# A ring of weight chunks in on-chip memory, laid out in the order 1, 2, 3, 0

## The chip, the cores and the metric

One core of a Trainium2 chip runs the kernel. The metric is the device time of one execution, in microseconds (us). TensorE is the matmul engine (PE in the profile, PEld its weight loads), VectorE is DVE, ScalarE is ACT, GpSimd is POOL, SyncE is SP.

## What is computed

A decoder block on 512 tokens (16 meta tokens go ahead, 528 in all) with model width 2048, all float32:

```
hn   = rms_norm(h)                       # 528 x 2048
proj = hn @ w_in                         # q k v z, b and a logits, p, gate_a gate_b
q, k, v = silu(conv(q, k, v)); gated delta rule over 8 heads -> o;  y_a = (norm(o) * silu(z)) @ w_proj_a
y_b  = (causal pools of p, mixed by pool_w, scaled) @ w_proj_b
h   += (sigmoid(gate_a) * y_a + sigmoid(gate_b) * y_b) @ w_out
h   += (silu(rms_norm(h) @ w_gate) * (rms_norm(h) @ w_up)) @ w_down
out  = rms_norm(h) of the 512 real tokens
```

## The kernel before

Each large product is made of three matmuls, since a float32 operand is split into two parts, a high one rounded to the fp32r type and a low one that holds the rest: high x high, high x low, low x high. The weights are the stationary operand of the projections; the tokens stream past them.

The token tiles are hn_hi and hn_lo, each [128, 16, 528] (16 tiles kt of 128 model channels, 528 tokens, lines 206 and 207). They lie behind each other from hn_at; one tile is 528 x 4 = 2112 bytes in each partition.

The projection weights come in chunks of 1024 floats a partition: 4 kt tiles x 256 output columns. A chunk passes through three places with four slots each (SLOTS = 4, the slot is the chunk's number modulo 4): SyncE loads it to w_raw (line 520), ScalarE copies it rounded to w_hi (line 935), VectorE subtracts w_hi from w_raw and writes w_lo (line 1378), TensorE reads w_hi and w_lo. When it is done with a chunk (the semaphore chunk_used) the slot is free. Chunk c of a unit of 256 output columns holds the tiles kt = c, c + 4, c + 8, c + 12. It gives 24 groups of work: 2 halves m of 128 output columns, 4 tiles, 3 products.

What TensorE does, in order, with the ring:

- the first unit of stage a (first_unit, line 2105), all chunks first with tokens 0 to 255 (256 columns), then, behind ab_products (line 2170, the same pairs of token parts with a stationary tile of 32 columns, ab_hl, which steps by 128 bytes from one kt to the next, from a multiple of 256 on), all chunks with tokens 256 to 527 (272 columns)
- stage a: 11 more units (q, k, v), chunk_products at line 2128; each weight tile meets the 256 and then the 272 columns (hn_halves)
- the gates: 16 units, real tokens only, 512 columns that begin 16 floats into a token tile (hn_real); pieces of eight such matmuls alternate with the small matmuls of the delta rule
- stage p: 4 units, 256 and 272 columns again
- stage z: 4 units, 512 columns
- the merge: 8 units of 4 chunks, 512 columns of o and zb. Its chunks are written to other tiles over the same memory, w_hi_m and w_lo_m (lines 1097, 1138, 1660, 1794). The tiles of o and zb begin at multiples of 256 bytes.

Later stages use the same memory for other tiles: out (its weights stream, line 2432 to 2434), the FFN (lines 2457 to 2459, 44 units of 7 products of 24 matmuls; weights hi_a, hi_b, hi_c and their low parts stand, the sums s_hi and s_lo with 256 columns stream, from s_at = hn_at + 64) and down. The weights of the FFN's third product, hi_2 and lo_2, begin at ext_at + 8192 from the fifth unit on and 64 bytes behind it in the first four (`two_at`, line 331). The asserts at lines 191, 209 and 219 say that whi_at, wlo_at, hn_at and ext_at are equal modulo 256 (BEAT).

The positions in the ring are set by the function ring. Before, slot i of w_hi begins at whi_at + 64 + 4160 i, slot i of w_hi_m at whi_at + 4096 i, and the same for w_lo.

Of the kernel before, what the change touches and what calls it, by code (L numbers as in the profile page):

```python
# [10 lines left out]
F32R = mybir.dt.float32r  # L11
# [3 lines left out]
P = 128  # L15
# [22 lines left out]
SLOTS = 4  # L38
CHUNK = 1024
# [101 lines left out]
def hybrid_block(nc, x, meta_tokens, norm_mix_w, w_in, conv_w, a_log, dt_bias, o_norm_w, w_proj_a, pool_w,  # L141
                 pool_scale, w_proj_b, w_out, norm_ffn_w, w_ffn_gate, w_ffn_up, w_ffn_down, norm_final_w, out):
    ctx = ExitStack()
    with ctx:
# [12 lines left out]
        top = [(nc.sbuf_base + 63) // 64 * 64]  # L157

        def place(name, shape, dtype=F32, at=None):
            size = int(np.prod(shape[1:])) * 4  # L160
            offset = top[0] if at is None else at
            if at is None:
                top[0] += (size + 63) // 64 * 64
            return nc.alloc_sbuf_tensor_at(name, shape, dtype, offset=offset)
# [2 lines left out]
        raw = [place(f"w_raw{i}", [P, CHUNK]) for i in range(SLOTS)]  # L167


        def ring(name, step, first):  # L170
            return [place(f"{name}{i}", [P, CHUNK], F32R, at=top[0] + first + (4 * CHUNK + step) * i) for i in range(SLOTS)]

        LINE = 64
        whi_at = top[0]
        whi, whi_m = ring("w_hi", LINE, LINE), ring("w_hi_m", 0, 0)
        top[0] += SLOTS * (4 * CHUNK + LINE)
        wlo_at = top[0]
        wlo, wlo_m = ring("w_lo", LINE, LINE), ring("w_lo_m", 0, 0)
        top[0] += SLOTS * (4 * CHUNK + LINE)

        minus_half = place("minus_half", [P, 16])
# [2335 lines left out]
```

## Time and profile before

| | us |
|---|---|
| median of 3 runs (2654.24 to 2655.65) | 2654.39 |
| the profiled execution | 2655.96 |
| its span | 2654.2 |
| TensorE busy | 2604.5 |
| VectorE busy | 1816.0 |
| ScalarE busy | 999.0 |
| GpSimd busy | 318.9 |

The span runs from the first to the last instruction. Matmuls overlap: one is on record for longer than the distance to the next (0.28 us of 256 columns, of which the next begins after 0.11 to 0.12), so the distance between starts is what counts. In the timeline, equal neighbours are merged: x2 is one of 256 and one of 272 columns.

### The profile page before, as it was taken

What the parts mean: (1) busy time and instruction counts of PE and PEld (TensorE: products, weight loads), DVE (VectorE), ACT (ScalarE), POOL (GpSimd) and SP (SyncE); (2) the same over time, 40 slices, a digit from 0 to 9 for tenths busy, and PEclk for the clock granted to TensorE, in tenths of its full rate; (3) what the DMA queues carried; (4) which work ended last, traced back from release to release, by engine and by line L of the source; (5) the groups of instructions that cost most, each with busy time, mean ns of one, the idle gap of its engine ahead of it and who ended that gap; (6) DMA issues with size and microseconds to landing.
All of it is one profiled execution on the core that took longest, in us unless ns stands there. A gap on an engine that the chain in (4) does not pass through costs nothing.

```text
span 2654.2 us, 43654 instructions
## 1 busy us (share of the span) xinstructions
PE 2604.5 (98%) x17278; PEld 2369.4 (89%) x17278; DVE 1816.0 (68%) x1714; ACT 999.0 (38%) x1016; POOL 318.9 (12%) x326
## 2 busy tenths in 40 slices
PE   7999999999999999999989999999999999999998
PEld 6999988888889977888879999999999998888886
DVE  5444555554543234558888888888888888888898
ACT  4443322222222232223454444444444444333334
POOL 6000034444431500100000000000000000000000
PEclk8999999999999999999999999999999999999999
DMA  4333333333333434689333444544454449866562
GB/s 145 98 87 95 84 87 88 91 83 91 88 90 92 110 87 165 231 282 324 127 138 124 161 155 148 173 153 156 147 179 150 154 150 344 279 198 218 161 203 102
DMA packets 346856, 400.84 MB, mean 151 GB/s; under 512 B 11626, under 2 KB 300563, under 8 KB 345619
## 3 DMA queue, kind: packets, MB, share of 16 engines
q1 hardware_dynamic: 287122, 335.39, 40.4%
q10 hardware_dynamic: 59664, 64.51, 7.1%
q8 instruction: 46, 0.75, 0.1%
q14 instruction: 24, 0.19, 0.0%
HBM read 328.02 MB, written 71.84 MB: 151 GB/s over the span
## 4 chain that ended last, share of the span: by engine, by line
PE 92%; DVE 3%; issue 1%; ACT 1%; DMA 1%; POOL 1%; SPq 0%; DVEq 0%; ACTq 0%; POOLq 0%
PE psum L2128 34%; PE psum L2457 10%; PE psum L2459 10%; PE psum L2458 10%; PE psum L2432 7%; PE psum L2433 6%; PE psum L2434 6%; PE psum L2286 2%; PE psum L2105 1%; PE psum L2297 1%; DMA w_raw<-in_w_proj_a 1%; PE psum L2372 1%; PE psum L2267 0%; DMA dn_raw<-in_w_ffn_down 0%; POOL hn_lo L766 0%
## 5 line engine op out<-in xcount | busy, mean ns | idle before, releaser
L2128 PE MATMUL psum<-hn_hi,w_hi 128*128 128x256 f32 (+1 forms) x1600 | 451.2, 331 | 0.0
L2128 PE MATMUL psum<-hn_lo,w_hi 128*128 128x256 f32 (+1 forms) x1600 | 450.0, 330 | 0.0
L2128 PE MATMUL psum<-hn_hi,w_lo 128*128 128x256 f32 (+1 forms) x1600 | 449.3, 330 | 0.0
L1378 DVE TENSOR_TENSOR w_lo<-w_raw,w_hi 128x1024 fp32r<-128x1024 f32 x144 | 190.1, 1321 | 260.7 <-ACT w_hi L935 259.7
L935 ACT ACTIVATE w_hi<-w_raw 128x1024 fp32r<-128x1024 f32 x144 | 152.2, 1058 | 415.8 <-PE psum L2128 387.6
L2128 PEld LDWEIGHTS psum<-hn_hi,w_hi 128*128 128x128 f32 x1600 | 271.0, 188 | 22.8 <-issue 0.2
L2128 PEld LDWEIGHTS psum<-hn_lo,w_hi 128*128 128x128 f32 x1600 | 270.8, 188 | 22.9 <-issue 0.7
L2128 PEld LDWEIGHTS psum<-hn_hi,w_lo 128*128 128x128 f32 x1600 | 270.5, 188 | 22.7
L2432 PE MATMUL psum<-dn_hi,act_hl 128*128 128x512 f32 x616 | 240.9, 391 | 2.0 <-DVE dn_lo L1712 2.0
L2434 PE MATMUL psum<-dn_hi,act_hl 128*128 128x512 f32 x616 | 240.3, 390 | 0.0
L2433 PE MATMUL psum<-dn_lo,act_hl 128*128 128x512 f32 x616 | 240.2, 390 | 0.0
L2457 PE MATMUL psum<-s_hi,hi_a 128*128 128x256 f32 x704 | 194.6, 276 | 1.0 <-DVE s_lo L1883 1.0
L2458 PE MATMUL psum<-s_lo,hi_a 128*128 128x256 f32 x704 | 194.4, 276 | 0.0
L2459 PE MATMUL psum<-s_hi,lo_a 128*128 128x256 f32 x704 | 194.4, 276 | 0.0
L2459 PE MATMUL psum<-s_hi,lo_b 128*128 128x256 f32 x704 | 194.4, 276 | 0.0
L2458 PE MATMUL psum<-s_lo,hi_c 128*128 128x256 f32 x704 | 194.4, 276 | 0.0
L2459 PE MATMUL psum<-s_hi,lo_c 128*128 128x256 f32 x704 | 194.4, 276 | 0.0
L2458 PE MATMUL psum<-s_lo,hi_b 128*128 128x256 f32 x704 | 194.4, 276 | 0.0
L2457 PE MATMUL psum<-s_hi,hi_c 128*128 128x256 f32 x704 | 194.4, 276 | 0.0
L2457 PE MATMUL psum<-s_hi,hi_b 128*128 128x256 f32 x704 | 194.4, 276 | 0.0
L920 POOL TENSOR_TENSOR rms<-rms_a,minus_half 128x1 f32<-128x1 f32 x4 | 2.6, 658 | 1281.9 <-DVE rms_a L2025 1281.9
L1185 ACT ACTIVATE hi<-t 128x1024 fp32r<-128x1024 f32 x44 | 46.8, 1064 | 267.9 <-DVE t L1829 267.9
(359 smaller groups left out, 6236.0 us busy)
## 6 DMA issues: line engine op xcount, KB each, us to landing
w_raw<-in_w_in SPq DMA_DIRECT2D x144, 512.0 KB, 3.9
ffn_raw<-in_w_ffn_gate SPq DMA_DIRECT2D x44, 1024.0 KB, 6.4
ffn_raw<-in_w_ffn_up SPq DMA_DIRECT2D x44, 1024.0 KB, 6.9
dn_raw<-in_w_ffn_down SPq DMA_DIRECT2D x32, 1024.0 KB, 8.3
act_hl<-act_dram SPq DMA_DIRECT2D x56, 512.0 KB, 9.1
act_dram<-comb_hi ACTq DMA_DIRECT2D x22, 896.0 KB, 4.2
act_dram<-comb_lo ACTq DMA_DIRECT2D x22, 896.0 KB, 6.2
out_raw<-in_w_out SPq DMA_DIRECT2D x16, 1024.0 KB, 10.9
```

The source lines that it names most:

```text
L935: act.activation(whi[s][:], raw[s][:], ACT.Copy).then_inc(S["hi_ready"], 1)
L1185: act.activation(two(hi_2s, n)[:], two(t2s, n)[:], ACT.Copy).then_inc(S["hi_ready"], 1)
L1378: dve.tensor_tensor(wlo[s][:], raw[s][:], whi[s][:].bitcast(F32), ALU.subtract).then_inc(S["lo_ready"], 1)
L2105: ins = pe.matmul(outs(m)[i], lhs, mv, start=kt == 0 and j == 0, stop=kt == KT - 1 and j == 2)
L2128: ins = pe.matmul(o, lhs, r, start=kt == 0 and i == 0, stop=kt == 4 * n_chunks - 1 and i == 2)
L2286: ins = pe.matmul(bank(1)[:, i, :], x[:, i, :], B[11][:, i, :], start=True, stop=True)
L2432: pe.matmul(out, a_hi, w_hi, start=start and i == 0, stop=False, skip_group_check=True)
L2433: pe.matmul(out, a_hi, w_lo, start=False, stop=False, skip_group_check=True)
L2434: ins = pe.matmul(out, a_lo, w_hi, start=False, skip_group_check=True, stop=i == k - 1 and (what in ("b21", "b22", "t4") or at_end and wha ...
L2457: pe.matmul(out, w_hi[:, k0 + k, :], s_hi[c][:, k, :], start=start and k == 0, stop=False, skip_group_check=True)
L2458: pe.matmul(out, w_hi[:, k0 + k, :], s_lo[c][:, k, :], start=False, stop=False, skip_group_check=True)
L2459: ins = pe.matmul(out, w_lo[:, k0 + k, :], s_hi[c][:, k, :], start=False, stop=stop and k == HEADS - 1, skip_group_check=True)
```

## The change

The function ring takes a list of four places instead of a step and a first offset. Modulo 256, the slots 0, 1, 2, 3 of w_hi and w_lo begin at 64, 128, 192, 0 before and at 192, 0, 64, 128 after. In memory the order of the slots is 1, 2, 3, 0 after. The tiles of the merge take the same order, at multiples of 256 bytes. No instruction is added, taken away or moved.

```diff
-        def ring(name, step, first):
-            return [place(f"{name}{i}", [P, CHUNK], F32R, at=top[0] + first + (4 * CHUNK + step) * i) for i in range(SLOTS)]
+        def ring(name, places):
+            return [place(f"{name}{i}", [P, CHUNK], F32R, at=top[0] + at) for i, at in enumerate(places)]
 
         LINE = 64
+        BEHIND = [(4 * CHUNK + LINE) * ((i + SLOTS - 1) % SLOTS) for i in range(SLOTS)]
+        EVEN = [3 * (4 * CHUNK) + 4 * LINE, 0, 4 * CHUNK, 2 * (4 * CHUNK)]
         whi_at = top[0]
-        whi, whi_m = ring("w_hi", LINE, LINE), ring("w_hi_m", 0, 0)
+        whi, whi_m = ring("w_hi", BEHIND), ring("w_hi_m", EVEN)
         top[0] += SLOTS * (4 * CHUNK + LINE)
         wlo_at = top[0]
-        wlo, wlo_m = ring("w_lo", LINE, LINE), ring("w_lo_m", 0, 0)
+        wlo, wlo_m = ring("w_lo", BEHIND), ring("w_lo_m", EVEN)
         top[0] += SLOTS * (4 * CHUNK + LINE)
```

## Rows read from the trace of the kernel before

**Rows 1.** The page: span, busy time of PE, granted clock in 40 slices.
```profile
span 2654.2 us, 43654 instructions
...
PE 2604.5 (98%) x17278; PEld 2369.4 (89%) x17278; DVE 1816.0 (68%) x1714; ACT 999.0 (38%) x1016; POOL 318.9 (12%) x326
...
PEclk8999999999999999999999999999999999999999
```

**Rows 2.** PE's waits from 68 to 1018 us (in total, times, longest).
```profile
PE psum L2286 <- DVE gdn L1582: 1.7, 1, 1.7
```

**Rows 3.** SP's longest wait; DVE's split (busy, mean ns, idle before it).
```profile
SPq L520 <- DVE w_lo L1378: 859.6, 142, 19.1
...
L1378 DVE TENSOR_TENSOR w_lo<-w_raw,w_hi 128x1024 fp32r<-128x1024 f32 x144 | 190.1, 1321 | 260.7 <-ACT w_hi L935 259.7
```

**Rows 4.** Groups of PE instructions by form; one of three products each.
```profile
L2128 PE MATMUL psum<-hn_hi,w_hi 128*128 128x512 f32 x640 | 256.8, 401 | 0.0
...
L2128 PE MATMUL psum<-hn_hi,w_hi 128*128 128x272 f32 x480 | 138.2, 288 | 0.0
...
L2128 PE MATMUL psum<-hn_hi,w_hi 128*128 128x256 f32 x480 | 134.1, 279 | 0.0
```

**Rows 5.** The chain that ended last: start us, us, what and how many.
```profile
47.49 7.70 PE psum L2170 x64
55.19 11.87 PE psum L2105 x96
...
68.27 215.55 PE psum L2128 x1792
```

**Rows 6.** The weight loads of L2128, one of three products.
```profile
L2128 PEld LDWEIGHTS psum<-hn_hi,w_hi 128*128 128x128 f32 x1600 | 271.0, 188 | 22.8 <-issue 0.2
```

**Rows 7.** Timeline of PE in the FFN's fourth unit: start us, length us.
```profile
1441.86 0.28 PE L2457 MATMUL psum<-s_hi,hi 128*128 128x256 f32 x1
...
1444.74 0.28 PE L2457 MATMUL psum<-s_hi,hi_b 128*128 128x256 f32 x1
...
1447.46 0.28 PE L2457 MATMUL psum<-s_hi,hi_b 128*128 128x256 f32 x1
```

**Rows 8.** The same in the fifth unit.
```profile
1461.06 0.28 PE L2457 MATMUL psum<-s_hi,hi 128*128 128x256 f32 x1
...
1463.78 0.28 PE L2457 MATMUL psum<-s_hi,hi_b 128*128 128x256 f32 x1
```

**Rows 9.** Timeline of PE in the first unit, last chunk, 256 columns.
```profile
45.17 0.28 PE L2105 MATMUL psum<-hn_hi,w_lo 128*128 128x256 f32 x1
...
47.21 0.28 PE L2105 MATMUL psum<-hn_hi,w_lo 128*128 128x256 f32 x1
```

**Rows 10.** L2128 alone in stage p: stretch, its length, PE busy (count).
```profile
823.70:916.10 92.40, 92.37 (x768) 1.00 0.40 108
```

**Rows 11.** Timeline of PE, ab_products, first matmul of kt = 4 to 8.
```profile
49.24 0.41 PE L2170 MATMUL psum<-hn_hi,ab_hl 128*32 128x256 f32 x2
...
49.73 0.40 PE L2170 MATMUL psum<-hn_hi,ab_hl 128*32 128x256 f32 x2
...
50.20 0.40 PE L2170 MATMUL psum<-hn_hi,ab_hl 128*32 128x256 f32 x2
...
50.69 0.40 PE L2170 MATMUL psum<-hn_hi,ab_hl 128*32 128x256 f32 x2
...
51.17 0.40 PE L2170 MATMUL psum<-hn_hi,ab_hl 128*32 128x256 f32 x2
```

**Rows 12.** Timeline of PE in stage z, before and behind a chunk's boundary.
```profile
918.18 0.39 PE L2128 MATMUL psum<-hn_hi,w_hi 128*128 128x512 f32 x1
...
921.58 0.39 PE L2128 MATMUL psum<-hn_hi,w_hi 128*128 128x512 f32 x1
...
924.34 0.39 PE L2128 MATMUL psum<-hn_hi,w_hi 128*128 128x512 f32 x1
```

## The prediction

> **What bounds the kernel now.** I read the page first, then TensorE's waits, then the spacing of matmuls inside single stages. The page has TensorE at 98% of the span, and the granted clock at its upper level (2.4 GHz) in all but the first slice [rows 1]. Between 68 and 1018 us, where every matmul that the change touches lies except the first unit, TensorE waits once, 1.7 us, for something the change doesn't touch [rows 2]. The engines that fill the ring have room: SyncE waited 860 us in all for w_lo before its loads, VectorE stood idle 260 us before its split [rows 3]. So the number to read is the spacing of consecutive matmuls. A saved or lost nanosecond there goes straight into the time, and nothing else on the path moves.
>
> Three forms of L2128 read the ring through whi and wlo: 640 x 3 matmuls of 512 columns (gates and z), and 480 x 3 each of 272 and of 256 columns, always in pairs (a and p) [rows 4]. With the first unit (L2105, 96 of 256 and 96 of 272 columns) that is 1920 wide ones, 1440 pairs and 192 single ones.
>
> I call **position** the start of a weight chunk minus the start of the token columns that stream during its use, modulo 256 bytes. A token tile has 528 floats, 2112 bytes, so tile kt begins 64 kt past hn_at. Chunk c holds tiles c, c+4, c+8, c+12, which all begin at 64 c. Columns and k blocks inside a chunk step by 512 and 1024 bytes and change nothing. Before, chunk c begins at 64 (c+1): position +64 for a, p and the first unit, and 0 for gates and z, whose columns begin 16 floats later. After, chunk c begins at 64 (c+3), that is 64 (c-1): position -64 for a and p, and 128 for gates and z. The merge tiles begin at multiples of 4096, or at 12544 = 49 x 256, so they stay at position 0. Each matmul has a weight load beside it [rows 6]; only this relation can change its speed, since shapes, counts, order, waits and DMAs are the same.
>
> **What the trace says about positions, at 256 columns.** The FFN shows the clean contrast. In the fourth unit the product of hi_2 uses tiles that begin 64 bytes past a multiple of 256, like the sums s: position 0. Its 24 matmuls take 1444.74 - 1441.86 = 2.88 us, 120.0 ns each; the 24 of hi_b behind them, at -64, take 2.72 us, 113.3 ns [rows 7]. One unit on, the same product reads tiles that begin at a multiple of 256, position -64, and takes 1463.78 - 1461.06 = 2.72 us, 113.3 ns [rows 8]. So position 0 costs 6.7 ns a matmul of 256 columns. Position +64 is in the first unit: 18 steps from 45.17 to 47.21, 113.3 ns [rows 9]. Hence -64 and +64 are equally good at 256 columns, and 0 is bad. Of 128 no row of full width tells.
>
> The Trainium skill (TensorE: Matmul & The Clock Gate, section Part 2: What happens when you issue a matmul) speaks against any effect: TensorE has two independent SBUF read ports, so loading the next tile's weights takes no read bandwidth from the running matmul. By that rule each term below is 0 and the time stays. Rows 7 and 8 disagree with its letter, 120.0 against 113.3 ns for the same line; for the terms below it happens to give the same sum.
>
> **Part 1, a and p: +64 to -64.** Stage a takes 215.55 us for 1792 matmuls, 240.6 ns a pair [rows 5]; stage p has 92.37 us for 384 pairs, 240.5 ns [rows 10]. At the FFN's rate (113.3 / 256 = 0.4427 ns a column) a pair of 528 columns would take 233.8 ns. So 6.8 ns a pair are over, 9.8 us in all, and the first unit's 272-column part (11.87 us / 96 = 123.6 ns [rows 5] against 120.4) has 0.3 us more. Does position hold them? The row nearest to this is ab_products, L2170: the same 256 + 272 pairs on the same tokens, with a load of 32 columns only and a position that walks through 0, 64, 128 and 192 with kt. It takes 7.70 us / 32 = 240.6 ns a pair [rows 5], as much as stage a to a tenth of a nanosecond, and its groups of two pairs take 0.49, 0.47, 0.49 and 0.48 us [rows 11]. With a quarter of the load and every position the excess is the same; it looks like a matter of alternating 256 and 272 columns. Value taken: 0. Bounds: -10.1 us (all of the excess goes), and above nothing: the group at 192 (that is -64) took 10 ns more than the one at 64, 5 ns a pair, 7.2 us for 1440 pairs. The reading is rounded to 10 ns, so it is a bound, not a value.
>
> **Part 2, gates and z: 0 to 128.** At position 0 a matmul of 512 columns, locked in, takes (921.58 - 918.18) / 15 = 226.7 ns [rows 12], exactly twice 113.3. So it shows none of the 6.7 ns that 256 columns pay at the same position. The simplest reading: a conflict delays the weight load, which fills the whole matmul at 256 columns and has half of it to spare at 512. Then 128, whether good or bad for the load, is hidden as well. Value taken: 0. Behind a chunk's boundary the spacing wobbles: (924.34 - 921.58) / 12 = 230.0 ns [rows 12], some 40 ns a chunk. Were that gone in all 80 chunks, -3.2 us. Upper bound: the 6.7 ns of rows 7 on each of 1920, +12.9 us. It isn't hidden by anything if the stream itself is what is delayed, since TensorE is the bound there.
>
> **Part 3, the rest: 0.** Scalar and vector splits write the same 1024 columns to other addresses and have room [rows 3]. The merge tiles only swap places. Loads go to raw, which doesn't move.
>
> **Sum.** The profiled execution took 2655.96 us, span 2654.2 and 1.8 around it, 1.6 above the median of 2654.39. 0 + 0 + 0 leaves 2655.96 for it and 2654.4 for the median.
>
> **The rivals.** (1) Faster: -64 is the position that the FFN's steady rate proves over hundreds of microseconds, and -64 alone is good in pairs too; the pairs fall to 233.8 ns, gates stay: 2654.4 - 10.1 = 2644.3. For it: rows 7 and 8. Against: rows 9 and the 240.6 ns of ab_products. (2) Slower, at the gates: position 128 falls on the same half of a 128-byte pattern as 0, or is worse, and at 512 columns it delays the stream itself. Price 12.9 us, 2667.3; it decides from 2.8 ns a matmul (5.3 us / 1920). For it: the wobble at chunk boundaries shows that wide matmuls aren't immune. Against: they are at twice 113.3 at position 0. (3) Slower, at the pairs: -64 is worse than +64 when 256 and 272 alternate, by the 5 ns of rows 11: 2661.6. (4) Both (1) and (2): -10.1 + 12.9 = 2657.2, within what can't be told from no change.
>
> **How the numbers follow.** No effect 0.37; (1) 0.22; (4) 0.08; (2) 0.20; (3) 0.13. Some 0.2% of this time (5.3 us) is what a measurement can tell from no change. Faster: 0.22. Same: 0.37 + 0.08 = 0.45. Slower: 0.20 + 0.13 = 0.33. The likeliest case gives 2654.4, with its own range of 2651 (wobble gone) to 2657. The 8-in-10 range takes in (1), (3) and nearly all of (2): 2644 to 2667.
>
> **What would show it.** In the changed profile: the spacing of a pair in stage p, 240.5 (forecast) or 233.8 ns (1) or above 245 (3); a locked 512-column matmul in z, 226.7 (forecast) or above 229.5 (2); the first unit's 256-column matmuls unchanged at 113.3, or part of the reading of rows 9 is wrong; the merge unchanged in any case. The forecast falls if the pair's excess belongs to the position after all, or if position 128 reaches the stream.

## The result and the profile after

The changed kernel takes 2667.2 us (median of 5 runs, 2666.06 to 2668.52); the kernel before, beside it on the same chip, 2655.65 (2654.24 to 2655.82). The ratio is 1.0046, with a 95% interval of 1.0034 to 1.0058: slower by 12 us, over twice what I had counted as no change. The forecast, no effect at 2654.4, was wrong, and the time lies just past the upper end of the range. In the changed kernel every line number from the ring on is higher by 2: L2128 is L2130, L2105 is L2107.

The page, which answers to [rows 1]:

```profile
span 2666.7 us, 43654 instructions
...
PE 2616.3 (98%) x17278; PEld 2377.7 (89%) x17278; DVE 1815.5 (68%) x1714; ACT 999.3 (37%) x1016; POOL 318.4 (12%) x326
```

The same instructions, the same work on VectorE, ScalarE and GpSimd. The span grew by 12.5 us and TensorE's busy time by 11.9. So TensorE didn't wait more, it was slower at the same work. Where, a view of stretches tells. Its columns are the stretch, its length, and then the busy time of PE, PEld, DVE, ACT and POOL, the granted clock, the DMA share and GB/s. The four stretches are stage a, the gates, stage p and stage z. First the kernel before:

```profile
68.27:328.45 260.18, 260.18 (x2155) 258.98 (x2156) 121.92 (x170) 100.12 (x119) 5.78 (x11) 1.00 0.34 92
328.45:823.70 495.25, 493.54 (x2785) 418.25 (x2784) 256.23 (x392) 128.86 (x182) 194.31 (x164) 1.00 0.32 88
823.70:916.10 92.40, 92.40 (x771) 92.40 (x770) 20.74 (x16) 21.87 (x25) 33.96 (x26) 1.00 0.40 108
916.10:1017.60 101.50, 101.50 (x418) 77.97 (x416) 39.13 (x43) 36.14 (x42) 15.68 (x12) 1.00 0.24 68
```

and the changed kernel:

```profile
70.02:336.10 266.08, 266.08 (x2156) 264.88 (x2156) 121.91 (x170) 100.09 (x119) 5.75 (x11) 1.00 0.34 90
336.10:834.70 498.60, 497.04 (x2787) 419.32 (x2785) 256.22 (x392) 128.99 (x182) 194.37 (x164) 1.00 0.31 87
834.70:928.10 93.40, 93.40 (x771) 93.40 (x769) 20.48 (x16) 21.84 (x25) 33.97 (x26) 1.00 0.39 107
928.10:1031.20 103.10, 103.10 (x418) 78.31 (x416) 40.17 (x43) 36.18 (x42) 14.61 (x12) 1.00 0.24 67
```

Stage a lost 5.9 us, the gates 3.35, p 1.0 and z 1.6: 11.85 of the 12.5. The granted clock is 1.00 in all eight rows, the upper level of 2.4 GHz, so the clock takes no part. The rest is small: +1.75 ahead of stage a and -1.1 behind z. Ahead of stage a the chain of waits has (start, us, what, how many) the following rows, first one of the kernel before, whose other rows are in [rows 5] (11.87 us for the 96), then those of the changed one:

```profile
40.14 7.35 PE psum L2105 x48
```

```profile
40.29 8.67 PE psum L2107 x48
...
56.67 12.14 PE psum L2107 x96
...
70.02 221.02 PE psum L2130 x1792
```

The 1.32 us of the first row belong to this one execution: the granted clock of that stretch was 0.65 against 0.77 before, and in three of the four other kernels below with the changed placement it took 7.45, in the fourth 5.92. Over all kernels here it took from 5.83 us, at a granted clock of 1.00, to 8.67, at 0.65. The second row's 0.27 us are an effect of position: with the other rotations the piece takes 12.06 to 12.14 too. Behind z, the merge was 0.7 us shorter, out 0.5 longer, the FFN 1.1 shorter and down 0.2 longer; the last section comes back to the FFN.

Inside the stages, the spacing of starts. A 512-column matmul in the locked part of stage z (position 128 now):

```profile
953.25 0.41 PE L2130 MATMUL psum<-hn_hi,w_hi 128*128 128x512 f32 x1
...
955.81 0.40 PE L2130 MATMUL psum<-hn_hi,w_lo 128*128 128x512 f32 x1
```

2.56 us for 11 steps, 232.7 ns, where [rows 12] had 226.7. (The rows are rounded to 10 ns, so a reading over 11 steps is good to about 1 ns.) A pair in stage a: 221.02 / 896 = 246.7 ns, where [rows 5] had 240.6. The 256-column matmuls of the first unit, where [rows 9] had 113.3:

```profile
47.15 0.28 PE L2107 MATMUL psum<-hn_lo,w_hi 128*128 128x256 f32 x1
...
48.68 0.28 PE L2107 MATMUL psum<-hn_hi,w_lo 128*128 128x256 f32 x1
```

1.53 us for 13 steps, 117.7 ns. But this isn't an effect of the change. The kernel before has 117.7 ns in the same unit too, in its chunk 1, at the position +64 that gave 113.3 in its last chunk:

```profile
34.26 0.28 PE L2105 MATMUL psum<-hn_lo,w_hi 128*128 128x256 f32 x1
...
36.85 0.28 PE L2105 MATMUL psum<-hn_hi,w_lo 128*128 128x256 f32 x1
```

2.59 us for 22 steps. In the changed kernel it is chunk 1 that takes 113.4. The merge, whose position didn't change, kept its 226.7 ns. Of the four signs that the prediction had named, the wide matmul fell out as in slower case (2) and the merge stayed, as it was to do in any case. The first unit's sign pointed at the reading of rows 9, and rightly: a single place doesn't give the rate. A pair in p came to 243.2 ns (93.4 / 384), between the 240.5 of the forecast and the 245 of rival (3).

### The profile page after: what moved, and what is told of

The parts are those of the page before. It is cut to its first block, busy times and chain, and to the rows that moved or that the text cites. A ratio compares the mean times of both kernels' runs of the same rounds, so it can differ in the third digit from the quotient of the medians.

```text
span 2666.7 us, 43654 instructions
## 1 busy us (share of the span) xinstructions
PE 2616.3 (98%) x17278; PEld 2377.7 (89%) x17278; DVE 1815.5 (68%) x1714; ACT 999.3 (37%) x1016; POOL 318.4 (12%) x326
## 4 chain that ended last, share of the span: by engine, by line
PE 92%; DVE 3%; issue 2%; DMA 1%; ACT 1%; POOL 1%; SPq 0%; DVEq 0%; ACTq 0%; POOLq 0%
PE psum L2130 35%; PE psum L2459 10%; PE psum L2461 10%; PE psum L2460 10%; PE psum L2434 6%; PE psum L2436 6%; PE psum L2435 6%; PE psum L2288 2%; PE psum L2107 1%; PE psum L2299 1%; DMA w_raw<-in_w_proj_a 1%; PE psum L2374 1%; PE psum L2269 0%; DMA dn_raw<-in_w_ffn_down 0%; PE psum L2255 0%
## 5 line engine op out<-in xcount | busy, mean ns | idle before, releaser
L2130 PE MATMUL psum<-hn_hi,w_hi 128*128 128x256 f32 (+1 forms) x1600 | 454.6, 333 | 0.0
L2130 PE MATMUL psum<-hn_lo,w_hi 128*128 128x256 f32 (+1 forms) x1600 | 454.5, 333 | 0.0
L2130 PE MATMUL psum<-hn_hi,w_lo 128*128 128x256 f32 (+1 forms) x1600 | 453.5, 332 | 0.0
L2130 PEld LDWEIGHTS psum<-hn_hi,w_hi 128*128 128x128 f32 x1600 | 271.0, 188 | 24.0 <-issue 0.2
L2130 PEld LDWEIGHTS psum<-hn_lo,w_hi 128*128 128x128 f32 x1600 | 271.0, 188 | 23.9 <-issue 0.7
L2130 PEld LDWEIGHTS psum<-hn_hi,w_lo 128*128 128x128 f32 x1600 | 270.8, 188 | 23.5
L2436 PE MATMUL psum<-dn_hi,act_hl 128*128 128x512 f32 x616 | 240.6, 391 | 0.0
L2435 PE MATMUL psum<-dn_lo,act_hl 128*128 128x512 f32 x616 | 240.5, 390 | 0.0
```

Source lines behind the costliest of these rows:

```text
L2130: ins = pe.matmul(o, lhs, r, start=kt == 0 and i == 0, stop=kt == 4 * n_chunks - 1 and i == 2)
L2435: pe.matmul(out, a_hi, w_lo, start=False, stop=False, skip_group_check=True)
L2436: ins = pe.matmul(out, a_lo, w_hi, start=False, skip_group_check=True, stop=i == k - 1 and (what in ("b21", "b22", "t4") or at_end and wha ...
```

## The experiments

The theory after the result: the relation of the two start addresses, of the standing weight tile and of the streaming columns, modulo 256 bytes, sets the spacing of matmuls, wide ones too. It acts alike for every tile with the same relation, whatever the slot or the stage. (The runs bear this out for the wide matmuls; the narrower ones turn out to have two rates at one relation.) The rivals: the order of the slots in memory (a neighbour of the slot being read is being written by ScalarE or VectorE), and for the pairs something in the alternation of 256 and 272 columns. Positions are named as in the prediction. Where a time stands without a ratio, it is one execution.

### Another rotation: pairs at 0, wide ones at -64

```diff
-        BEHIND = [(4 * CHUNK + LINE) * ((i + SLOTS - 1) % SLOTS) for i in range(SLOTS)]
-        EVEN = [3 * (4 * CHUNK) + 4 * LINE, 0, 4 * CHUNK, 2 * (4 * CHUNK)]
+        BEHIND = [(4 * CHUNK + LINE) * i for i in range(SLOTS)]
+        EVEN = [4 * CHUNK * i for i in range(SLOTS)]
```

> Ring in the order 0, 1, 2, 3 from whi_at on: slot i begins at 64 i modulo 256. Position (start of the chunk minus start of the streamed columns, modulo 256) is then 0 for a and p and -64 for gates and z; the merge stays at 0. Theory P (the position of the weight load against the stream sets the spacing): the pairs at 0 are the worst or equal to the changed kernel's, 246 ns or more (each 256-column matmul at 120 or above), and gates and z differ from the 226.7 ns that z reaches at 0. Rival W (what matters is where ScalarE and VectorE write the split parts, not the load's position): as positions move by the same step as the write addresses, pairs and wide matmuls should move together and no table by position comes out. Rival S (a state left by the start of a stage, not the layout): pairs at 240 or 246 without relation to the position.

Measured: 2662.76 us, ratio 1.0024 (1.0014 to 1.0034). The four stretches, in the same order:

```profile
68.75:332.40 263.65, 263.65 (x2155) 262.45 (x2156) 121.92 (x170) 100.08 (x119) 5.76 (x11) 1.00 0.33 90
332.40:828.60 496.20, 494.52 (x2785) 418.35 (x2785) 256.30 (x392) 128.79 (x182) 194.31 (x164) 1.00 0.31 87
828.60:922.20 93.60, 93.60 (x771) 93.60 (x770) 20.48 (x16) 21.83 (x25) 33.97 (x26) 1.00 0.39 107
922.20:1024.20 102.00, 102.00 (x418) 78.09 (x417) 39.78 (x43) 36.16 (x42) 15.63 (x12) 1.00 0.23 67
```

Against before: +3.5, +0.95, +1.2 and +0.5, together 6.1 of the 7.5 us between the medians. The slots lie here in the order 0, 1, 2, 3, as before; only each begins 64 bytes earlier, and all four stages are slower. So it isn't the order in memory. The pairs came to 243.9 ns in stage a (218.55 us for 1792 matmuls), less than the 246 or more that was expected and less than the changed kernel's 246.7. In stage z the spacing is

```profile
952.57 0.39 PE L2130 MATMUL psum<-hn_hi,w_hi 128*128 128x512 f32 x1
...
955.09 0.40 PE L2130 MATMUL psum<-hn_hi,w_lo 128*128 128x512 f32 x1
```

2.52 / 11 = 229.1 ns for wide matmuls at -64, and in the first unit, at 0,

```profile
46.03 0.28 PE L2107 MATMUL psum<-hn_hi,w_lo 128*128 128x256 f32 x1
...
47.47 0.28 PE L2107 MATMUL psum<-hn_hi,w_lo 128*128 128x256 f32 x1
```

1.44 / 12 = 120.0 ns, the number that [rows 7] had for position 0 in another stage, with other tiles.

### The merge gets positions too, pairs at 128, wide ones at +64

```diff
-        BEHIND = [(4 * CHUNK + LINE) * ((i + SLOTS - 1) % SLOTS) for i in range(SLOTS)]
-        EVEN = [3 * (4 * CHUNK) + 4 * LINE, 0, 4 * CHUNK, 2 * (4 * CHUNK)]
+        BEHIND = [(4 * CHUNK + LINE) * ((i + 2) % SLOTS) for i in range(SLOTS)]
+        EVEN = BEHIND
```

> Ring in memory order 2, 3, 0, 1: slot i begins at 64 i + 128 modulo 256. Position 128 for a and p, +64 for gates and z. The merge reads the same tiles, so its chunks stand at 128, -64, 0 and +64 in turn, each with 512 columns. Theory P: a third value for the pairs; the merge's four chunks separate by position, 0 at 226.7 ns and 128 at about 231 to 233 as gates and z show in the changed kernel. Rival S: all four chunks of the merge alike.

Measured: 2672.69 us, ratio 1.0063 (1.0046 to 1.0080), the slowest of all. Stages a, gates, p, z and, fifth, the merge (176.10 us before):

```profile
68.64:334.90 266.26, 266.26 (x2155) 265.06 (x2156) 121.86 (x170) 100.14 (x119) 5.77 (x11) 1.00 0.33 90
334.90:834.20 499.30, 497.77 (x2787) 418.40 (x2785) 256.22 (x392) 129.02 (x182) 194.43 (x164) 1.00 0.30 87
834.20:928.90 94.70, 94.70 (x771) 94.70 (x769) 20.35 (x16) 21.84 (x25) 34.20 (x26) 1.00 0.38 106
928.90:1032.20 103.30, 103.30 (x418) 77.78 (x416) 40.03 (x43) 36.21 (x43) 14.56 (x12) 1.00 0.23 66
1032.20:1210.60 178.40, 177.44 (x769) 144.35 (x769) 90.53 (x104) 45.76 (x42) 18.00 (x14) 1.00 0.74 251
```

+6.1, +4.05, +2.3, +1.8 and +2.3: 16.5 of the 17.4 us between the medians. The merge, untouched by every other kernel here, is slower as soon as its tiles leave position 0. Its four chunks stand at 128, -64, 0 and +64, and the starts give 231.7, 228.9, 226.6 and 233.5 ns (from the 13th to the 24th matmul of each, in the unit from 1100 us on). They agree within 1 ns with what z showed at the same positions: 232.7 at 128, 229.1 at -64, 226.7 at 0.

### All four positions in every stage

```diff
-        BEHIND = [(4 * CHUNK + LINE) * ((i + SLOTS - 1) % SLOTS) for i in range(SLOTS)]
-        EVEN = [3 * (4 * CHUNK) + 4 * LINE, 0, 4 * CHUNK, 2 * (4 * CHUNK)]
+        BEHIND = [4 * CHUNK * i for i in range(SLOTS)]
+        EVEN = BEHIND
```

> All slots at multiples of 256 in all stages. Chunk c stands at -64 c for a and p and at -64 (c + 1) for gates and z. Theory P: within one stage the spacing differs by chunk: in a, chunk 3 (+64) at 240 ns a pair, chunk 1 (-64) near 246; in z, chunk 3 (0) at 226.7, chunk 1 (128) near 232. Rival S: the four chunks of a stage are alike.

Measured: 2664.45 us. Every slot begins at a multiple of 256 bytes, so the position goes through all four values within a unit. This is the cleanest of the runs, because one execution compares them side by side. Timeline of stage z, second halves of chunks 0 to 3 of one unit (-64, 128, +64, 0):

```profile
948.89 0.39 PE L2130 MATMUL psum<-hn_hi,w_hi 128*128 128x512 f32 x1
...
951.41 0.39 PE L2130 MATMUL psum<-hn_hi,w_lo 128*128 128x512 f32 x1
...
954.43 0.39 PE L2130 MATMUL psum<-hn_hi,w_hi 128*128 128x512 f32 x1
...
956.99 0.40 PE L2130 MATMUL psum<-hn_hi,w_lo 128*128 128x512 f32 x1
...
960.03 0.39 PE L2130 MATMUL psum<-hn_hi,w_hi 128*128 128x512 f32 x1
...
962.60 0.39 PE L2130 MATMUL psum<-hn_hi,w_lo 128*128 128x512 f32 x1
...
965.57 0.39 PE L2130 MATMUL psum<-hn_hi,w_hi 128*128 128x512 f32 x1
...
968.06 0.39 PE L2130 MATMUL psum<-hn_hi,w_lo 128*128 128x512 f32 x1
```

Each pair of rows spans 11 steps: 2.52, 2.56, 2.57 and 2.49 us, which is 229.1, 232.7, 233.6 and 226.4 ns; averaged over the four units of z, 229.0, 232.7, 233.4 and 226.7. The pairs of stage a, averaged by chunk over the first nine units (2nd to 24th pair of each chunk), take 243.9 ns (0), 243.5 (-64), 246.7 (128) and 240.3 (+64). For wide matmuls 0 is the best position and +64 the worst, 0.7 ns behind 128; for pairs +64 is the best and 128 the worst. The kernel before has each where it is best. For the pairs at -64 some 246 were expected, and they are 3 ns below the changed kernel's 246.7; the run with another entry, below, takes this up.

### Positions that aren't multiples of 64

```diff
-        whi, whi_m = ring("w_hi", LINE, LINE), ring("w_hi_m", 0, 0)
+        whi, whi_m = ring("w_hi", LINE, LINE // 2), ring("w_hi_m", 0, 0)
-        wlo, wlo_m = ring("w_lo", LINE, LINE), ring("w_lo_m", 0, 0)
+        wlo, wlo_m = ring("w_lo", LINE, LINE // 2), ring("w_lo_m", 0, 0)
```

(on the kernel before: pairs at +32, wide ones at -32)

> The kernel before with w_hi and w_lo 32 bytes lower: slot i at 32 + 64 i modulo 256, position +32 for a and p and -32 for gates and z. Theory P: gates and z lie between those at 0 (226.6) and at -64 (229.2) or at either; pairs between 240.3 (+64) and 243.8 (0). Slower than before by 1 to 6 us.

Measured: 2669.08 us, ratio 1.0055 (1.0038 to 1.0071). Stage a's piece of the chain, and stage z:

```profile
67.18 220.52 PE psum L2128 x1792
...
957.40 0.39 PE L2128 MATMUL psum<-hn_hi,w_hi 128*128 128x512 f32 x1
...
959.97 0.39 PE L2128 MATMUL psum<-hn_hi,w_lo 128*128 128x512 f32 x1
```

246.1 ns a pair and 2.57 / 11 = 233.6 ns. The kernel is 13.6 us slower than the one before, where 1 to 6 were expected: the guess that a place in between costs no more than its neighbours was wrong. A shift of 32 bytes from the best places costs as much as the worst multiples of 64. So a place 32 bytes off a good one isn't good, and at these two nothing is to be won.

### Without most of the split's writes

In both split functions, on the changed kernel and on the kernel before (4 columns of most chunks are written instead of 1024, so most of the split of the weights is left out):

```diff
+                n = CHUNK if isinstance(g, int) and not G_GATES <= g < G_MERGE - 4 else 4
-                act.activation(whi[s][:], raw[s][:], ACT.Copy)...
+                act.activation(whi[s][:, 0:n], raw[s][:, 0:n], ACT.Copy)...
```

> The changed kernel, in which ScalarE and VectorE split only 4 of the 1024 columns of a chunk in every loop unit (a but its first and last two units, gates, p, z, merge): that part of the computation is left out. Theory P: the spacing stays, 246 ns a pair and about 232 ns for 512 columns. Rival W: with the writes gone the pairs fall to 240 ns and the wide ones to 226.7.

> The kernel before, in which ScalarE and VectorE split only 4 of the 1024 columns of a chunk in every loop unit: that part of the computation is left out. The question is the wobble behind each chunk's boundary in z. Theory P (position of loads alone): it stays, about 230 ns in the first half of a chunk and 226.6 in the second, since the load of the next chunk's first tile stands at +64. Rival W (the splits, which run just then, disturb the stream): the first half falls to 226.7.

Measured: 2663.68 us on the changed kernel and 2652.35 on the one before. Stage a of the changed kernel, then of the one before:

```profile
68.91 221.02 PE psum L2132 x1792
```

```profile
68.20 215.55 PE psum L2130 x1792
```

To a hundredth of a microsecond what they were with all writes (221.02 above, 215.55 in [rows 5]), though VectorE's busy time in the changed kernel's stage a fell from 122 to 81 us and ScalarE's from 100 to 67. In the gates ScalarE's busy time fell from 129 to 75 us and VectorE's from 256 to 184, and the difference between the two kernels stayed: 11.3 us, against 11.6 with all writes. So the rival of the split's writes beside reads falls. (The DMA's writes to w_raw went on as before and weren't tried.) The wobble behind a chunk's boundary stays as well in the quiet kernel before (230.2 ns in the first half of a chunk of z, 226.6 in the second), so it isn't theirs either.

### 256 columns alone in a and p

On both kernels the 272 columns are cut to 256 in chunk_products, so the last 16 tokens of q, k, v and p are left out:

```diff
                             for o, r in zip(outs(m), mv):
+                                if len(mv) == 2:
+                                    o, r = o[:, 0:EARLY], r[:, 0:EARLY]
                                 ins = pe.matmul(o, lhs, r, ...
```

> The kernel before; in the loop units of a and in p the second part of a pair streams 256 columns instead of 272, so the last 16 tokens' projections are left out. Position +64. If the 6.8 ns of excess a pair come from the alternation with 272 columns, the pairs fall to 226.7 ns (two at 113.3), saving 13.7 ns on 1440 pairs, 19 us. If they belong to the position, the 256-column matmuls stay at 116 or more.

> The same with the changed kernel, position -64. If -64 is as good as +64 once only 256 columns are in play (what I read out of the FFN before), the pairs fall to 226.7 ns as well. If -64 has a second, slower rate (118 ns, which the first unit of the changed kernel shows), the pairs stay at 236.

Measured: 2645.82 us (+64) and 2652.64 (-64). Stage a is the same in both, 211.32 us for 1792, 117.9 ns each: neither the 113.3 of [rows 9] nor different. In stage p of the kernel before, the first matmul of four chunks in a row, 48 matmuls each:

```profile
839.02 0.40 PE L2130 MATMUL psum<-hn_hi,w_hi 128*128 128x256 f32 x2
...
844.48 0.40 PE L2130 MATMUL psum<-hn_hi,w_hi 128*128 128x256 f32 x2
...
850.13 0.40 PE L2130 MATMUL psum<-hn_hi,w_hi 128*128 128x256 f32 x2
...
855.59 0.40 PE L2130 MATMUL psum<-hn_hi,w_hi 128*128 128x256 f32 x2
```

5.46, 5.65 and 5.46 us: 113.8, 117.7 and 113.8 ns. One kernel, one position, one shape, and two rates in turn: in all sixteen chunks of p, chunks 0 and 2 of a unit at the lower rate and 1 and 3 at the higher. Stage a has the same slots and ran at 117.8 in all chunks of its first nine units, so the slot alone doesn't decide. This is what the prediction lacked, though the first unit of the kernel before showed both rates. Matmuls of 256 columns at +64 or -64 have two rates, 113.3 and 117.7, and a single row of either says only which one was on. In the changed version all of p ran at 117.8. The step from +64 to -64 costs nothing in stage a here and 6 ns a pair with 272 columns between.

### The alternation taken apart

On the kernel before: first, all 256-column matmuls of a half chunk and then all its 272-column ones; second, two parts of 264.

```diff
-                    for k in range(4):
+                    for part, k in ((part, k) for part in range(len(outs(m))) for k in range(4)):
...
-                            for o, r in zip(outs(m), mv):
-                                ins = pe.matmul(o, lhs, r, ...
+                            ins = pe.matmul(outs(m)[part], lhs, mv[part], ...
```

> The kernel before, with the order of matmuls within half a chunk changed: the 12 of 256 columns first, then the 12 of 272, instead of in turn. Same matmuls, same loads, position +64. The first unit ran them apart at 113.3 and 123.6 ns, 236.9 against 240.5 a pair. Theory A (alternation costs): 3.6 x 1440 = 5.2 us faster, about 2650. Rival: the 272-column matmul carries the cost wherever it stands, and the 256-column one stays at 116: no change.

```diff
-EARLY = 256
+EARLY = 264
```

> The kernel before with tokens split 264 + 264 instead of 256 + 272 in the first unit, a and p. The second half begins 1056 bytes on, so that its position is 32 bytes lower than the first's (+64 and +32). Theory P with a step of 64 bytes: about 240 ns a pair, no change. If the unequal lengths cost the excess: 233.8 to 236 ns, 6 to 9 us faster. If positions in between two lines are worse: 244 or more, 5 us slower or more.

Measured: 2655.04 us, ratio 0.9998 (0.9989 to 1.0008), and 2655.78, ratio 1.0001 (0.9991 to 1.0011). Stage a's piece, of the first and of the second:

```profile
69.35 214.80 PE psum L2127 x1792
```

```profile
67.49 215.56 PE psum L2128 x1792
```

239.7 and 240.6 ns a pair, where [rows 5] had 240.6. With equal parts of 264 columns the excess of 6.8 ns over the FFN's rate stays, to a hundredth of a microsecond in the piece. The lengths don't alternate there (the positions do, +64 and +32, since the second part begins 1056 bytes on). With the parts taken apart the lengths don't alternate from one matmul to the next either, and only 0.9 of the 6.8 ns went. By the starts, runs of twelve then take 115.9 ns at 256 columns and 123.6 at 272, the 123.6 of the first unit's second part. So nearly half of the excess belongs to the 272 columns wherever they stand, as the expectation's rival said, and the prediction's "matter of alternating 256 and 272 columns" is refuted. Neither version beats the kernel before.

### A load of a quarter

On the changed kernel, for the wide matmuls of gates and z, 32 weight columns instead of 128 (three quarters of their output channels are left out):

```diff
+                                if moving is hn_real:
+                                    o, lhs = o[0:32], lhs[:, 0:32]
```

> The changed kernel; in the gates and in z each load takes 32 columns of the weights instead of 128 and each matmul writes 32 partitions, so three quarters of these products are left out. Position 128, 512 columns stream as before. If the load's reads are what holds the stream up, the excess of some 6 ns over 226.7 shrinks with the load, to about 1.5 (228 ns). If the address of the stream alone, or its order, is the cause, z stays at 232.5. If my prediction's picture were right (only the load is delayed, and it has time to spare), there would have been no excess to begin with.

Measured: 2665.05 us. In z, at 128:

```profile
953.32 0.40 PE L2132 MATMUL psum<-hn_hi,w_hi 128*32 128x512 f32 x1
...
955.86 0.39 PE L2132 MATMUL psum<-hn_hi,w_lo 128*32 128x512 f32 x1
```

2.54 / 11 = 230.9 ns. The load on record went from 188 to 106 ns (median), and the excess over 226.7 from 6.0 to 4.2. Were the excess in proportion to the weight columns, 1.5 would be left. So the load seems to have a part in it, since a smaller one takes away a third, but not by its size alone. The run can't tell the narrower load from the narrower result, for each matmul also writes 32 partitions instead of 128. What the rest is stays open.

### Another entry to stage a

On the changed kernel, the last small matmul ahead of stage a is issued once more:

```diff
+            ins = pe.matmul(PS[:, 6, 2 * HEADS * CH:2 * HEADS * (CH + 1)], src, both[:], start=True, stop=True)
             ins.then_inc(S["ab_done"], 1)
```

> The changed kernel with the last of the ten small matmuls before stage a's loop made twice, nothing else. At the same position -64 stage a shows 246.1 ns a pair in the changed kernel, but stage p 243.2, and the 256-column matmuls at -64 and +64 show 113.3 or 117.8. If which of two rates holds is set by the moment of entry, stage a can now come out at 243; if stage a's rate belongs to the stage (tiles, addresses), it stays at 246.

Measured: 2665.90 us. Stage a:

```profile
68.90:331.90 263.00, 263.00 (x2155) 261.80 (x2155) 121.59 (x169) 99.98 (x119) 5.76 (x11) 1.00 0.33 90
```

3.1 us less than in the changed kernel, with the same addresses. Its piece of 1792 took 218.04 us, 243.3 ns a pair, the number of stage p of the changed kernel (93.4 / 384 = 243.2). By the starts of single forms, the distance behind a 256-column matmul went from 122.5 to 118.9 ns, the one behind a 272-column matmul from 124.1 to 124.3. So of the 5.9 us of stage a, 2.8 belong to position -64 in its better state (263.0 against 260.2), and 3.1 to the state in which the stage was entered. The gates, p and z were as in the changed kernel. The whole execution is only 1.3 us below the changed kernel's median, since in the FFN the lower rate set in a unit later than there (0.8 us) and other stretches differ by some tenths.

## Why the prediction was wrong

**What bounds the kernel** was right. TensorE is the bound, every nanosecond of spacing went into the time, and no wait was added. The waits, the splits and the DMAs took no part.

**Which stages and which relation** was right. Of what the edit touches, position sets the spacing: the order in memory and the place of the writes don't. The three rotations and the shift by 32 bytes moved just the stages whose positions they moved. What was missing is that at 256 columns, and in pairs, a position has more than one rate. The Trainium skill (TensorE: Matmul & The Clock Gate, section Part 2: What happens when you issue a matmul) says that two independent read ports keep a load from taking bandwidth from the running matmul. By that the place of the weight tile wouldn't matter to the running matmul. The trace disagrees: matmuls of one shape in one stage take 226.4 or 233.6 ns by the relation of the two starts. Whether it is read bandwidth that they lose, no run here shows.

**Part 2, gates and z, value 0.** This is the step that failed first. From 226.7 = 2 x 113.3 at position 0 I concluded that a conflict delays only the load, which has time to spare at 512 columns. But the row was at position 0, and 0 is the position at which wide matmuls pay nothing. Position 0 is bad for 256 columns (120.0 against 113.3) and good for 512: the ranking turns round with the width, so the one can't be carried over to the other. At 128 a wide matmul takes 232.7 ns, 6.0 more. That is near the 6.7 of the upper bound, yet the two stages lost 4.95 us and not 12.9. The reason is the wobble: before, the mean over the 1201 distances within the pieces of the gates was already 229.9 ns and not 226.7, and 228.3 in z, since the matmuls behind a break or a chunk's boundary are slower. After, it is 232.5 in both. The two excesses don't add, and the mean rose by 2.6 ns (gates, 3.2 us) and 4.2 (z, 1.6 us). Rival (2) was right that wide matmuls slow down at 128, at a price 2.6 times too high; which access is delayed (it said "the stream itself") no run shows. Had its 233.4 ns (226.7 + 6.7) been set against these means and not against 226.7, the price would have been 3.5 x 1201 + 5.1 x 384 ns, 6.2 us.

**Part 1, pairs, value 0.** Three links broke. "-64 and +64 are equally good at 256 columns" was read from rows that each showed one of two rates. The prediction's own sign for this came true, the last chunk of the first unit went from 113.3 to 117.7, but by luck: with 256 columns alone in a and p, the same chunk ran at 117.8 at +64 as well. Then ab_products: its 240.6 ns, the same as stage a's, was taken to mean that position doesn't matter. It stays 240.6 in every kernel with 256 + 272 columns (7.70 to 7.71 us), but it has a small load and a mean over four positions, and the full-width tiles in the run with all four positions spread from 240.3 to 246.7. Equal sums over different things showed nothing. Its groups [rows 11] weren't flat either: averaged over kt = 4 to 14 of the kernel before, a pair takes 241.7 ns at 0, 238.8 at +64, 242.0 at 128 and 240.8 at -64, +64 the best and 128 the worst as with full-width tiles. The 5 ns that the rounded rows gave between -64 and +64 are 2 there; the sign was right. The pairs lost 6.1 ns in stage a and 2.7 in p, 5.9 + 1.0 = 6.9 us, where rival (3) had 7.2. That these are so near is luck too: 3.1 of the 6.9 hang on the state in which stage a was entered.

**Part 3, the rest, 0** was right, and the merge stayed. The first unit, whose second part the prediction had counted under part 1, lost 0.27 us in its 272-column part, 126.5 ns against 123.6.

**The cases.** Rivals (2) and (3) were both true at once, and I had listed each alone and no sum of them. Had I combined them as (1) and (2) were combined in (4), the bounds would have reached 2654.4 + 7.2 + 12.9 = 2674.5, and the measured 2667.2 would have lain inside. The near hit of rival (2)'s 2667.3 is a coincidence: it is 4.95 from the gates and z and 6.9 from the pairs. The faster case had no support in any run: no position gave a pair of 256 and 272 columns 233.8 ns, the least was 239.7.

What the runs leave open: which accesses meet at which position, why a quarter of the load, with a quarter of the result, takes only a third of the excess away, and what chooses between the two rates.

## What to carry to other kernels

Where TensorE is the bound and its operands' addresses move, read the spacing of starts for each shape at each relation of the two start addresses modulo 256, and don't carry a ranking from one width to another. In an unknown case one kernel whose slots go through all the relations ranks them side by side in one trace. If two slow cases touch different stages, their sum is a case as well. And a rate read in one place should be looked for in a second place before it is called the rate of that shape.

## What the runs showed of the hardware

Spacing in ns by position, with tiles of 128 weight columns (wide: mean over the second halves of all chunks of stage z, from the unrounded starts; pairs: pieces of stage a, in brackets stage p where it differs):

| position | 512 columns | 256 + 272 | kernel |
|---|---|---|---|
| 0 | 226.7 | 243.9 | before; first rotation |
| -64 | 228.7 | 246.7 (243.2) | first rotation; changed |
| +64 | 233.4 | 240.6 | second rotation; before |
| 128 | 232.9 | 246.6 | changed; second rotation |
| +32 | not run | 246.1 | shift by 32 |
| -32 | 233.3 | not run | shift by 32 |

Not expected either: the two rates at 256 columns, 113.3 and 117.7 ns, with the same tiles, position and clock, lasting for hundreds of matmuls. The FFN of the kernel before has both. In its second unit, the product of hi_2 (position 0) and the first and 19th matmul of hi_b behind it:

```profile
1402.83 0.28 PE L2457 MATMUL psum<-s_hi,hi 128*128 128x256 f32 x1
...
1405.71 0.28 PE L2457 MATMUL psum<-s_hi,hi_b 128*128 128x256 f32 x1
...
1407.83 0.28 PE L2457 MATMUL psum<-s_hi,hi_b 128*128 128x256 f32 x1
```

2.12 us for 18 steps, 117.8 ns, at the position that takes 113.3 in [rows 7]. The lower rate began at 1425.54, right behind the product of hi_2 of the third unit. In the changed kernel it began behind the same product of the second unit, 20.4 us sooner after the FFN's start; at 4.5 of 117.8 ns that is 0.8 of the FFN's 1.1 us. In stage p with 256 columns alone it changed from chunk to chunk at one and the same position. The pairs at -64 have two rates as well: 246.7 ns in stage a of the changed kernel, 243.3 with one more matmul ahead of it. What sets it was not tried, apart from the one extra matmul ahead of stage a, which shows that the entry can decide.
